# Moving the gate pieces of a mixture-of-experts layer to a second DMA queue

## What is computed

```python
hid = jax.nn.silu(xblk @ w_gate[e]) * (xblk @ w_up[e])   # w_gate[e], w_up[e]: 1024 x 512
return hid @ w_down[e]                                     # w_down[e]: 512 x 1024
```

## Time and profile before

| | us |
|---|---|
| median of three runs | 901.25 |
| the profiled execution | 898.9 |
| its span | 897.0 |
| TensorE busy in it | 747.6 (83%) |
| VectorE busy | 375.3 (42%) |
| ScalarE busy | 168.3 (19%) |

### The profile page before, as it was taken

The page is one execution under the profiler, slowest core; times in us unless marked ns, Lnnn a source line. Parts: engine busy times, 40 slices in busy tenths (PEclk is TensorE's granted clock), DMA queues, the critical chain, the costliest instruction groups (busy, mean ns, idle before and its releaser), DMA issues.

```text
span 897.0 us, 13084 instructions
## 1 busy us (share of the span) xinstructions
PE 747.6 (83%) x5393; PEld 433.8 (48%) x5393; DVE 375.3 (42%) x884; ACT 168.3 (19%) x473; POOL 40.5 (5%) x36
## 2 busy tenths in 40 slices
PE   7999899999999899999999967666767585867765
PEld 4544664456467644446467644333434253334332
DVE  2478667657755676765452221112121111121113
ACT  3231730223355401141120110000000000001001
POOL 1110000012500000001000000000000000000000
PEclk9999999999999999999999998879798887698889
DMA  9984505766001839997799999999999999999994
GB/s 341 394 304 161 188 1 220 281 225 213 1 1 31 310 117 308 392 409 276 290 326 420 419 429 429 428 429 429 426 430 427 427 430 428 427 430 429 426 427 200
DMA packets 56140, 284.38 MB, mean 317 GB/s; under 512 B 2977, under 2 KB 7713, under 8 KB 43937
## 3 DMA queue, kind: packets, MB, share of 16 engines
q1 hardware_dynamic: 56096, 283.81, 79.1%
HBM read 282.75 MB, written 1.05 MB: 316 GB/s over the span
## 4 chain that ended last, share of the span: by engine, by line
PE 53%; DMA 36%; DVE 5%; ACT 2%; issue 1%; POOL 1%; SPq 1%; DVEq 0%; POOLq 0%
DMA ring<-in_up_w 31%; PE banks L2052 15%; PE banks L1900 9%; PE banks L2466 9%; PE banks L2298 4%; DMA ring<-in_down_w 3%; PE banks L2004 3%; PE banks L1932 2%; DMA ring<-in_ada_w 2%; PE banks L2521 2%; PE banks L1979 1%; POOL rs L629 1%; PE banks L2030 1%; DVE soft L1141 1%; PE banks L1878 1%
## 5 line engine op out<-in xcount | busy, mean ns | idle before, releaser
L2466 PE MATMUL banks<-ring,QT 128*32 128x256 f32 x1696 | 152.6, 470 | 61.3 <-DMA ring<-in_up_w 61.3
L2052 PE MATMUL banks<-ring,hT 128*128 128x512 f32 (+4 forms) x384 | 157.6, 565 | 1.8 <-DMA ring<-in_ab_w 1.7
L2466 PEld LDWEIGHTS banks<-ring,QT 128*32 128x32 f32 x1696 | 75.6, 130 | 115.2 <-issue 55.2
L2052 PEld LDWEIGHTS banks<-ring,hT 128*128 128x128 f32 x384 | 72.3, 193 | 74.9 <-issue 68.2
L1784 DVE TENSOR_TENSOR QT<-QT,banks 64x256 f32<-64x256 f32 x32 | 13.5, 423 | 216.4 <-ACT QT L984 216.4
L1793 DVE TENSOR_TENSOR QT<-banks,MOD 32x256 f32<-32x256 f32 x128 | 53.8, 421 | 107.2 <-PE banks L2521 105.9
L1900 PE MATMUL banks<-ring,hT 128*128 128x512 f32 x192 | 83.9, 594 | 1.9 <-ACT hT L669 1.8
L2521 PE MATMUL banks<-ring,QT 128*32 128x256 f32 x968 | 62.9, 400 | 14.5 <-ACT QT L991 11.9
L2466 PE MATMUL banks<-probs,QT 128*32 128x256 f32 x256 | 42.5, 501 | 36.0 <-DMA ring<-in_up_w 36.0
L629 POOL TENSOR_TENSOR rs<-st,mhalf 128x1 f32<-128x1 f32 (+7 forms) x27 | 33.3, 1237 | 851.0 <-DVE st L1830 440.1
L984 ACT ACTIVATE QT<-banks 64x256 f32<-64x256 f32 x32 | 12.0, 375 | 315.4 <-PE banks L2466 315.4
(11 more groups left out here) (369 smaller groups left out, 768.5 us busy)
## 6 DMA issues: line engine op xcount, KB each, us to landing
ring<-in_down_w SPq DMA_DIRECT2D x29, 2048.0 KB, 22.7
ring<-in_up_w SPq DMA_DIRECT2D x29, 2048.0 KB, 23.4
ring<-in_gate_w SPq DMA_DIRECT2D x22, 2048.0 KB, 20.4
ring<-in_ada_w SPq DMA_DIRECT2D x12, 2048.0 KB, 15.3
probs<-in_gate_w SPq DMA_DIRECT2D x8, 2048.0 KB, 27.4
ring<-in_ab_w SPq DMA_DIRECT2D x4, 2048.0 KB, 20.0
ring<-in_cd_w SPq DMA_DIRECT2D x4, 2048.0 KB, 13.4
ring<-in_in_w SPq DMA_DIRECT2D x4, 2048.0 KB, 16.0
```

The source lines that it names most:

```text
L2052: ins = pe.matmul(bank[b][:, 0:n], hT[:, k, t * P:(t + 1) * P], w[:, k, :], start=(k == 0), stop=(k == KD - 1))
L2466: return pe.matmul(bank[1][CAP * j:CAP * j + CAP, 0:256], XG[:, k, CAP * s:CAP * s + CAP], wk[:, :, 2 * (j % 2):2 * (j % 2) + 2], start=(k ...
```

## The change

The gate pieces from gate 5 on leave SyncE's list and are issued by ScalarE, on ScalarE's own DMA queue, by a new helper `load_gate`. It stands right behind `gathered_silu(e)`, ahead of `take_hidden(e)`: after expert e's silu, gate e + 2 (for e from 3 to 29, but not where e % 4 == 0), and where e % 4 == 2 also gate e + 4, which goes to `probs`. No wait on `g_gu` stands with them, since `gathered_silu(e)` has waited for it. The order of the up and down pieces on SyncE's queue stays as it was.

```diff
@@ the loads of the expert stage, SyncE
-                load_gathered(3, 5, 1)
                 load_gathered(4, 5, 1)
-                load_gathered(0, 6, 2)
                 load_gathered(5, 5, 3)
                 for e in range(6, NE - 2):
-                    for j in range(1 if e == 6 else 0, 3):
-                        once_in_four = e % 2 == 0 and j == 0
-                        load_gathered(3 * (e % 2) + j, e, e - 4 if once_in_four else e - 2)
+                    for j in (1, 2):
+                        load_gathered(3 * (e % 2) + j, e, e - 2)
                 for e in (NE - 2, NE - 1):
-                    for j in range(2):
-                        load_gathered(3 * (e % 2) + j, e, e - 4 if e % 2 == 0 and j == 0 else e - 2)
+                    load_gathered(3 * (e % 2) + 1, e, e - 2)
                 load_gathered(2, NE - 2, NE - 4)
@@ the expert stage, ScalarE
+                def load_gate(e):
+                    if e == 8:
+                        act.wait_ge(*upto("fifth_early", 96))
+                    home = probs if e % 4 == 2 else ring[eslot(3 * (e % 2))]
+                    act.dma_start(home[:, :].rearrange("p (k n) -> p k n", k=KD),
+                                  gate_w[bass.ds(e, 1), :, :].rearrange("e (p k) f -> p (e k) f", k=KD))\
+                       .then_inc(sem("ahead0" if e % 4 == 2 else f"slot{eslot(3 * (e % 2))}"), 16)
+
                 for e in range(NE):
                     gathered_silu(e)
+                    if e % 4 != 0 and 3 <= e < NE - 2:
+                        load_gate(e + 2)
+                    if e % 4 == 2 and e + 4 < NE:
+                        load_gate(e + 4)
                     take_hidden(e)
```

## The result

The changed kernel takes 903.89 us (median of 20 runs, 901.77 to 907.11), the kernel before 900.46 us (20 runs, 897.88 to 903.35). The ratio is 1.004, with a 95% interval of 1.003 to 1.005: 3.4 us slower by the medians. That is no change by the prediction's bound of 0.5%, but a difference all the same, since the interval leaves out 1. The forecast was 901.5 us, the range 896.5 to 908.

A forecast was written before the change was run, and what follows sets the result against it. The prediction took the stage as bound by its DMA stream of 2 MB pieces. 898.9 (profiled execution) + 0 + 0.3 for the end = 899.2 us; with the median 2.35 us above, 901.5 us, range 896.5 to 908.

The forecast's parts named there:

- The stream: Stage of 2 MB pieces at 428 GB/s: never idle under the new order, ending with the same last byte; worth 0.
- ScalarE's issues: 27 gate issues of 0.33 to 0.43 us between silu and `take_hidden`, fitting into ScalarE's idle 1.23 us; worth 0.
- Gate 5: Issued at 492.4 instead of 480.05 us, the stream staying fed and the piece landing in time for its round; worth 0.
- Gates 8 and 10, TensorE falls back: Gate 8 later, gate 10 15 us earlier; up and down pieces land 4 to 9 us later, TensorE likewise; worth 0.
- Gates in `probs` land in 10 to 20 us: Sign expected in the new profile: time from issue to landing of these gates, where the median was 27.4.
- The small share: Slower rival: ScalarE's queue gets under 0.41 of the engines, gates come late, 23 to 33 us lost; 7%.
- Rate: DMA rate while both queues are filled, about 265 us: taken as unchanged, worth 0, bounds -4.9 and +9.6 us.
- gain of rate: Faster rival: two queues gain rate or fill small gaps, 896.6 us; 8%.
- The end: Last experts: up 30 lands up to 4.9 us later, `down` of expert 30 starts 0 to 1.6 us later; +0.3 taken.
- The chances: Forecast 75%, four rivals 7, 7, 8 and 3%; the range said to leave out some 17%.
- the rate rival: Slower rival: two queues cost rate, at the bound of 413 GB/s +9.6 us, 911 us; 7%.

The follow-up runs named there:

- e1: The changed kernel with only gate 31 back on SyncE's queue, ahead of up 31: 901.09 against 899.48 us for the kernel before, ratio 1.0014.
- e6: The changed kernel with gates 29, 30 and 31 back on SyncE's queue: 900.02 against 899.70 us for the kernel before, ratio 1.0002.
- e2: The kernel before with gate 31 alone moved to ScalarE's queue: 902.43 against 899.48 us for the kernel before, ratio 1.0029.
- e3: The changed kernel with expert 31's gate/up round not split in halves: 900.91 against 899.48 us for the kernel before, ratio 1.0019.

## Why the prediction was right, and where it was off

**The stream** (the main step): right. It was to be full and end with the same bytes whatever the order; DMA share 1.01, 427 against 428 GB/s, 56.6 MB on the second queue as worked out, down 31 complete at about 885.0 us where it was 884.3, with the 0.85 us of the later start in it.

**ScalarE's issues**: right, worth 0. The timeline of the changed kernel for expert 3, to be held against the earlier trace rows:

```profile
492.80 0.38 ACT L980 ACTIVATE QT<-banks 64x256 f32<-64x256 f32 x1 [5.77 <-PE banks L2474]
492.80 0.34 ACTq L997 DMA_DIRECT2D ring<-in_gate_w  x1
494.40 0.28 ACT L987 ACTIVATE QT<-banks 128x128 f32<-128x128 f32 x1 [1.23 <-PE banks L2506]
```

The issue took 0.34 us and lies beside the silu, and the wait of 1.23 us ahead of the copy is to the hundredth what it was.

**Gate 5**: right. It was issued at 492.80 (beside the silu of expert 3, not behind it as I had put it), and its round ended in time for the issue at 510.99, which is 510.16 and the 0.85 us by which all of this execution is later.

**Gates 8 and 10, TensorE falls back**: right in kind and size. Up 8 landed at 519.60 + 29.34 = 548.9 us instead of 540.8, 8 us later (4 to 9 were given). "Gates in `probs` land in 10 to 20 us" was wrong, 24.3 in the median. Gate 10 was issued at 520.00 and landed 26.6 us later, at 546.6. It stands on its queue behind the rest of gate 7 (landed at 525.7) and behind gate 8 (at 536.8); after that each piece took some 10 us, about twice the 4.9 us that it has with the engines to itself.

**The small share**: didn't come. The queues' shares of the engines in the changed kernel between 700 and 712 us, when both had work:

```profile
q1 hardware_dynamic: 174, 2.59, 50.7%
q10 hardware_dynamic: 173, 2.57, 50.4%
```

Half each, above the 0.41 from which gates would have come late. By the Trainium skill ("DMA: Bandwidth & Descriptors", Queues, rings and completion order) each DMA engine serves the queues that have work in turn, packet by packet; these rows agree, as to the shares.

**Rate**: right at 0 within what can be told. From 470 to 500 us the changed kernel's rates are 411 and 413 where they were 413 and 425, and from 530 us on 1 GB/s less; e1's remainder of 1.3 us may come from that or be nothing, while e6 has 24 gates and 0.2 us. It stays open. No gain of rate either: the Trainium skill ("DMA: Bandwidth & Descriptors", Specifications) puts the ceiling at 435 GB/s, and with a second queue the rate stayed at 427.

**The end**: the step that was off, +0.3 taken from 0 to 1.6, measured +3.5. What made the size wrong is the price of the last gate/up round. It was put at 5.5 us, as any round at the lower clock, though the kernel writes it in two halves; it took 8.92. The trace of the kernel before could have told: the very same round took 6.58 us there at the full clock. From its start at 875.3 a round of 5.5 us would have ended at 880.8, and the 880.9 of the prediction's sum would have been met; the measured end is 884.2, 3.3 us later.

That the sum had the start of this round right, 875.4 (880.9 less 5.5) for 875.28, is luck, for it had the wrong path to it. It made up 30 late, with its round until 875.0 at the lower clock. But up 30, issued at 851.1, landed some 14 us later at 865.2, with gate 31 beside it only for the last 3.6 us, and its round was over at 869.2 (it is late in e2, where nothing has fallen back). What the round of expert 31 waited for was gate 31. "Gate 31 and up 31 are released together, before at 854.60" was carried over as if the time held after; they are released at 861.55, 6 us later beyond the common shift, since expert 29's round comes later. I had TensorE falling back in the paragraph just before, and forgot it here. And that two pieces released together on two queues land together, where on one queue gate 31 came 4.9 us ahead, stands nowhere in the sum. By e1 this is most of what costs, and not the late release: there gate 31 is released as late and lands at 870.6.

So the forecast of the total, 901.5 us for 903.9, is near because the stream, which is nearly all of the stage, was right; the term for the end measured 3.5 us, more than twice the 1.6 that was its upper bound.

**The chances**: the range is said to leave out some 17%. The rivals that it leaves out add up to the 7% of the small share and a part of the rate rival's 7%, so less than 14% by the prediction's own figures.

## What to carry to other kernels

In a stage that the DMA stream bounds, as this one, the order of transfers cost nothing that could be told until the last few pieces (e6); there, work through the order piece by piece, from the time at which each buffer comes free in the changed schedule, and price what stands behind each landing by its own code. If loads are spread over two queues, keep the last pieces, whose order was made so that the last byte has the least work behind it, on one queue: e6 does so and loses nothing that could be told. A round split so as to hide its first half behind a transfer is a loss when the two transfers are made to land together: here the split form took 6.58 us at the full clock where the whole one took 3.84, so it needs 2.7 us of waiting to hide in before it gains anything.

## What the runs showed of the hardware that I hadn't expected

ScalarE's DMA issue doesn't wait for the end of the silu that stands ahead of it: the two start within 0.01 us of each other (492.80 both). Whether an issue would hold up an instruction that is ready right behind it isn't shown, since ScalarE always had to wait for the turning next (1.23 us and more).

The price of an idle stretch just before a long round: behind 4.5 us of waiting for gate 31 TensorE had a granted clock of 0.50 from 875 to 880 us, and the split round took 8.92 us where it took 6.58 at 1.00 in the kernel before. In e3 the whole round, behind such a wait, took 5.49 us where one at 1.00 took 3.84. So the idle stretch costs 1.7 to 2.3 us here, and the split 2.7 us at the full clock and 3.4 where the round begins at the lower one.
